# Gate products and squares of the first branch group moved into the last sampled sequence, and four first halves of the last down products ahead of the second halves, in a hybrid MLA and Mamba-2 decoder layer

## The reference, cut to what matters

```python
# sampled sequences: attention over 4096 cached positions, in the latent space
o_lat = (einsum('bhtk,bkc->bthc', p_past, past_ckv) + einsum('bhts,bsc->bthc', p_new, c_kv_new))
o = einsum('bthc,chd->bthd', o_lat, w_uv)
# Mamba-2 branch: gate, then RMS norm in 4 groups of 512 features
yg = (y * silu(z)).reshape(B, T, SSM_GROUPS, D_INNER // SSM_GROUPS)
yg = rms_norm(yg, ssm_norm_g, 1e-5)
merged = g_a * (attn @ w_branch_a) + g_b * (ssm_out @ w_branch_b)
mix = merged @ w_out
h = layer_norm(ALPHA * x + mix, ln1_g, ln1_b)
# feed-forward network and the last norm
y = layer_norm(ALPHA * h + (silu(h @ w_gate) * (h @ w_up)) @ w_down, ln2_g, ln2_b)
```

## Time and profile before

| | before |
|---|---|
| median of 3 runs | 2912.71 us (2912.24 to 2912.79) |
| the profiled execution's own time | 2923.22 us |
| its span, first to last instruction | 2921.4 us |
| PE busy | 2829.9 us, 97% of the span |
| DVE busy | 1477.7 us, 51% |
| ACT, POOL busy | 736.8 us and 1015.3 us, 25% and 35% |
| mean granted TensorE clock | 0.979 of full speed |

### The profile page before, as it was taken

How to read it: one execution, slowest core, us unless ns; L and a number is a source line. 1 busy time by engine, 2 the same in 40 slices (tenths; PEclk the granted TensorE clock), 3 DMA queues, 4 the chain that set the end, 5 groups by cost and what they waited for, 6 DMA issues and landing times.

```text
span 2921.4 us, 45631 instructions
## 1 busy us (share of the span) xinstructions
PE 2829.9 (97%) x18894; PEld 2533.1 (87%) x18894; DVE 1477.7 (51%) x2052; ACT 736.8 (25%) x1154; POOL 1015.3 (35%) x603
## 2 busy tenths in 40 slices
PE   7999999999999999999999889999899999999998
PEld 7999999899999984555766589999799999999997
DVE  3535778766666655555344347865652222222226
ACT  2111211454454544454323222010120000000000
POOL 3443334333333314444211123444333333333331
PEclk9999999999999998999999989999899999999999
DMA  4263223565656544222343334353211111111111
GB/s 142 73 197 119 81 85 121 177 168 150 173 162 171 147 138 120 65 65 69 148 184 129 116 129 140 111 182 106 66 37 44 44 45 49 43 43 50 43 50 60
DMA packets 314769, 309.72 MB, mean 106 GB/s; under 512 B 32101, under 2 KB 273002, under 8 KB 312138
## 3 DMA queue, kind: packets, MB, share of 16 engines
q1 hardware_dynamic: 252392, 196.02, 23.7%
q10 hardware_dynamic: 58650, 73.89, 7.5%
q0 software_dynamic: 3584, 37.75, 3.4%
HBM read 229.41 MB, written 78.20 MB: 105 GB/s over the span
## 4 chain that ended last, share of the span: by engine, by line
PE 81%; DVE 11%; ACT 3%; issue 3%; DMA 1%; POOL 1%; ACTq 0%; SPq 0%; POOLq 0%; DVEq 0%
PE ps L969 41%; PE ps L1150 12%; PE ps L1284 4%; DVE cv L2237 3%; PE ps L1308 2%; PE ps L1298 2%; PE ps L1442 2%; PE ps L1418 2%; PE ps L1398 2%; DVE cv L2231 1%; PE ps L1183 1%; PE ps L1187 1%; PE ps L1176 1%; PE ps L1647 1%; DVE cv L2239 1%
## 5 line engine op out<-in xcount | busy, mean ns | idle before, releaser
L776 POOL TENSOR_TENSOR whi<-raw,cst 128x1024 fp32r<-128x1024 f32 x160 | 311.2, 1945 | 1154.1 <-PE ps L969 945.1
L778 POOL TENSOR_TENSOR wlo<-raw,whi 128x1024 fp32r<-128x1024 f32 x160 | 433.0, 2706 | 12.5
L969 PE MATMUL ps<-ahi,whi 128*128 128x352 f32 x1728 | 375.7, 325 | 2.1 <-POOL wlo L778 1.4
L969 PE MATMUL ps<-alo,whi 128*128 128x352 f32 x1728 | 375.9, 326 | 0.0
L969 PE MATMUL ps<-ahi,wlo 128*128 128x352 f32 x1728 | 372.6, 324 | 0.0
L969 PEld LDWEIGHTS ps<-ahi,whi 128*128 128x128 f32 x1728 | 294.7, 189 | 2.7 <-POOL wlo L778 1.7
L969 PEld LDWEIGHTS ps<-ahi,wlo 128*128 128x128 f32 x1728 | 296.9, 190 | 0.0
L969 PEld LDWEIGHTS ps<-alo,whi 128*128 128x128 f32 x1728 | 295.7, 189 | 0.0
L1150 PE MATMUL ps<-xhi,whi 128*128 128x352 f32 x768 | 255.9, 333 | 0.4 <-ACT xraw L1751 0.4
L1150 PE MATMUL ps<-xhi,wlo 128*128 128x352 f32 x768 | 247.9, 323 | 0.0
L1150 PE MATMUL ps<-xlo,whi 128*128 128x352 f32 x768 | 247.7, 323 | 0.0
(11 more groups left out here) (368 smaller groups left out, 5034.0 us busy)
## 6 DMA issues: line engine op xcount, KB each, us to landing
raw<-in_w_in SPq DMA_DIRECT2D x61, 512.0 KB, 5.0
s_a<-d_acum SPq DMA_DIRECT2D x32, 512.0 KB, 7.3
d_xbc<-so ACTq DMA_DIRECT2D x24, 528.0 KB, 2.7
gt<-d_g SPq DMA_DIRECT2D x24, 528.0 KB, 3.6
raw<-in_w_ffn_gate SPq DMA_DIRECT2D x22, 512.0 KB, 3.8
raw<-in_w_ffn_up SPq DMA_DIRECT2D x22, 512.0 KB, 3.7
raw<-in_w_ffn_down SPq DMA_DIRECT2D x22, 512.0 KB, 3.5
d_z<-zo ACTq DMA_DIRECT2D x16, 528.0 KB, 4.8
```

The source lines that it names most:

```text
L776: pool.tensor_tensor(whi[s][:, :], raw[:, u], ones[:, 0:1].broadcast_to([P, UNIT]), ALU.mult).then_inc(sem("unit_hi"), k["unit_hi"].adds(1))
L778: pool.tensor_tensor(wlo[s][:, :], raw[:, u], whi[s][:, :].bitcast(F32), ALU.subtract).then_inc(sem("unit_split"), k["unit_split"].adds(1))
L969: last = pe.matmul(ps[0:m, 3 * b + c, 0:width], w(j), x[:, j, at:at + width], start=i == 0, stop=i == n - 1)
```

## The change

The gate products of the first group are made by DVE inside the last sequence, after its copies of `prt` and before it waits for `olat_ready`; the sums of squares are taken right after `oseq`, before it waits for `end_turned`. So that the squares have room while `prt` is still read, `prt` and `oseq` lie further up in memory, and ACT waits with the fourth square (`murow`, which still lies over `prt`) for the eighth `olat_ready`. In the tail TensorE makes the first half (weight unit 0) of the token tiles 0 to 3 before it waits for the second weight unit, and the waits for free banks stand apart, ahead of the tiles that need them.

```diff
@@ memory
-    prb, prt = ar("prb", [P, NBK + 1, P]), ar("prt", [P, NBK + 1, P])
+    prb = ar("prb", [P, NBK + 1, P])
+    at_prt = ar.at + 704
+    ar = Arena(at_prt)
+    prt = ar("prt", [P, NBK + 1, P])
     oseq = ar("oseq", [P, NB, KL])
@@ PE, tail
-        def last_down(i):
+        def last_half(i, s):
             n = P if i < 8 else NS
             at, bank = slice(i * P, i * P + n), (6, 0, 2, 4)[i % 4]
-            if i >= 4:
-                pe.wait_ge(sem("tile_read"), k["tile_read"].next())
-            for s in range(2):
-                if i == 0:
-                    pe.wait_ge(sem("unit_split"), k["unit_split"].next())
-                for m in range(6):
...
-            if i == 0:
-                for b in range(2):
-                    pe.wait_ge(sem(f"res_free{b}"), k[f"res_free{b}"].next())
...
+        pe.wait_ge(sem("unit_split"), k["unit_split"].next())
+        last_half(0, 0)
+        pe.wait_ge(sem("res_free0"), k["res_free0"].next())
+        last_half(1, 0)
+        last_half(2, 0)
+        pe.wait_ge(sem("res_free1"), k["res_free1"].next())
+        last_half(3, 0)
+        pe.wait_ge(sem("unit_split"), k["unit_split"].next())
         for i in range(9):
-            last_down(i)
+            if i >= 4:
+                pe.wait_ge(sem("tile_read"), k["tile_read"].next())
+                last_half(i, 0)
+            last_half(i, 1)
+            sum_onto(i)
@@ ACT, squares
                 act.wait_ge(sem(f"yt_free{j % 2}"), k[f"yt_free{j % 2}"].next())
+                if g == 0 and j == 3:
+                    act.wait_ge(sem("olat_ready"), NB)
                 act.activation(sq4[j], yz[:, j], ACT.Square)...
@@ DVE, in sequence(b, q, more)
+            if not more and stop >= 7:
+                gated(0, 4)
             dve.wait_ge(sem("olat_ready"), k["olat_ready"].next())
@@ DVE, after the last sequence
+        if stop >= 7:
+            add_pairs()
+            add_all()
         dve.wait_ge(sem("end_turned"), k["end_turned"].next())
...
-        if stop >= 7:
-            gated(0, 4)
-            add_pairs()
-            add_all()
         dve.wait_ge(sem("os_ready"), k["os_ready"].next())
```

More of the change, by code:

```diff
@@ L438, in build @@
     assert ar.at >= at_g
+    assert ar.at + 3 * TOK * 4 <= at_prt
     srow, sq2, murow, rsrow = ar("srow", [P, TOK]), ar("sq2", [P, 2, TOK]), ar("murow", [P, TOK]), ar("rsrow", [P, TOK])
@@ L1633, in _, with sum_onto @@
         pe.wait_ge(sem("f_split"), k["f_split"].next(2))
-        def last_down(i):
+        def last_half(i, s):
             n = P if i < 8 else NS
             at, bank = slice(i * P, i * P + n), (6, 0, 2, 4)[i % 4]
-            if i >= 4:
-                pe.wait_ge(sem("tile_read"), k["tile_read"].next())
-            for s in range(2):
-                if i == 0:
-                    pe.wait_ge(sem("unit_split"), k["unit_split"].next())
-                for m in range(6):
-                    j, part = divmod(m, 3)
-                    w, x = ((whi, fhi), (whi, flo), (wlo, fhi))[part]
-                    pe.matmul(ps[0:n, bank + s, :], x[:, j, at], w[s][:, j * 512:(j + 1) * 512], start=m == 0, stop=False)
-            if i == 0:
-                for b in range(2):
-                    pe.wait_ge(sem(f"res_free{b}"), k[f"res_free{b}"].next())
+            for m in range(6):
+                j, part = divmod(m, 3)
+                w, x = ((whi, fhi), (whi, flo), (wlo, fhi))[part]
+                pe.matmul(ps[0:n, bank + s, :], x[:, j, at], w[s][:, j * 512:(j + 1) * 512], start=m == 0, stop=False)
+        def sum_onto(i):
+            n = P if i < 8 else NS
+            at, bank = slice(i * P, i * P + n), (6, 0, 2, 4)[i % 4]
             for e in range(KT):
@@ L2509, in keys_out, with gated @@
             dve.tensor_copy(dst, ps[:, 4 + i % 3, :].rearrange("p (r n) -> p r n", n=P)).then_inc(sem("keys_read1"), k["keys_read1"].adds(1))
+        def gated(j0, j1):
+            for j in range(j0, j1):
+                dve.wait_ge(sem(f"yt_full{j % 2}"), k[f"yt_full{j % 2}"].next(32))
+                dve.tensor_tensor(yz[:, j], yt[j % 2][:, :], gt[j % 2][:, :], ALU.mult).then_inc(sem(f"yt_free{j % 2}"), k[f"yt_free{j % 2}"].adds(1))
         def sequence(b, q, more):
@@ L2559, in _ @@
         sequence(1, NB - 1, False)
[L2560 to L2564, removed]
         def add_pairs():
```

## The result

| | before | after |
|---|---|---|
| median | 2912.47 us (2909.58 to 2912.79, 4 runs) | 2894.70 us (2890.39 to 2900.22, 4 runs) |
| ratio | | 0.9939, 95% interval 0.9926 to 0.9951 |
| the profiled execution's own time | 2923.22 us | 2900.22 us |
| its span | 2921.4 us | 2898.4 us |
| mean granted TensorE clock | 0.979 | 0.980 |

The changed kernel is 17.8 us faster (14.3 to 21.5). Later comparisons on four other chips gave less than 17.8, as the experiments show. In two of them the changed kernel has one disturbed execution (3290 us in after_again, 10144 us in after_third), which medians and ratios leave out.

What follows compares the result with a forecast made beforehand. TensorE, busy 97% of the span, was taken as the bound, with gains only where it waits or runs at lower clock. Hand-over 8.5 plus tail 2.6 makes 11.1 us, from 2912.7 to 2901.6 us; range 2895.5 to 2905.5.

Steps and rivals of the forecast that it cites:

- The base: Starting time: median 2912.7 us, with the profiled execution 10.5 us above it; gains carried over unchanged.
- Step 1: Hand-over, VectorE's order: the division waits behind the fourth gate product and its load, starting 1.5 us later.
- Step 2: Hand-over at full clock: the half unit ends at 1685.2 instead of 1699.06, a gain of 13.8 us.
- Step 3: Hand-over, TensorE's clock: falls about the middle of L1480, costing 5.25 us, so the first part gains 8.5 us.
- sign for a fallen clock: In the changed profile, L1480's count of 32 takes 4.5 to 6 us if the clock fell.
- Rival A: The clock holds through the hand-over: gain 16.4 us, time 2896.3 us; chance 0.20.
- Passed on whole: Behind the half unit everything waits by the same distances, so the shift reaches the end whole; 1.7 us either way for clock.
- Step 4: Tail: first halves fill the 3.12 us wait, then DVE sets the pace at 4.28 us a tile; gain 2.6 us.
- B: Less is passed on: clock down longer (hand-over gains 4, not 8.5) or tail keeps its pace; 2904 to 2908 us; chance 0.21.
- C: Hand-over: the fourth tile lands late and DVE holds up everything behind it; slower than before; chance 0.02.
- D: Hand-over: first two tiles not there at 1657.6, or additions wait for ACT's last square; 2910.1 us; chance 0.04.

Runs made afterwards that it cites:

- after_again: The changed kernel, nothing edited, run again on chip 9: median 2908.26 us, ratio 0.9954 to the kernel before.
- after_third: The changed kernel, nothing edited, run again on chip 4: median 2907.18 us, ratio 0.9953 to the kernel before.
- fourth_later: The changed kernel with the fourth gate product behind the division and two of three additions behind the copies of olat: 2899.17 us, ratio 0.9928 to before.
- after_fourth: The changed kernel, nothing edited, run again on chip 1: median 2895.08 us, ratio 0.9949 to the kernel before.
- after_fifth: The changed kernel, nothing edited, run again on chip 15: median 2895.34 us, ratio 0.9951 to the kernel before.
- before_filled: The kernel before plus 48 unread matmuls ahead of the group's sums, where TensorE idles: median 2913.87 us, ratio 1.0008 to the kernel before.
- fourth_later2: The kernel of fourth_later, nothing edited, run again on chip 1: median 2897.66 us, ratio 0.9956 to the kernel before.
- first_only: The kernel before with only the hand-over changed (gate products, additions, memory, ACT's wait), tail as before: median 2910.88 us, ratio 0.9963.
- before_again: The kernel before, nothing edited, run again on chip 15: median 2911.81 us, ratio 1.0002.
- memory_only: The kernel before with only prt and oseq moved further up in memory: median 2921.49 us, ratio 1.0002.
- after_filled: The changed kernel with eight and four unread matmuls in TensorE's two hand-over gaps: median 2906.44 us, ratio 0.9954 to the kernel before.

## Why the prediction was right or wrong

**The base.** The profile of before came from an execution with 30.0 us per sequence, its three timed runs have the median of chips with 28.4. That fits most of the 10.5 us between them (medians of the two kinds of chip differ by 9 to 10.6), which the prediction left unexplained and carried over unchanged. This was right, since neither place lies in the sequences' repeated part.

**Step 1, the order of VectorE.** Right in kind. The fourth tile landed 1655.44 - 1645.94 = 9.5 us after the first product's start (forecast 9.6). The division was 1.0 us late in the first profile and 0 to 1.2 in the six, where 1.5 was forecast. The Trainium skill (TensorE: Matmul & The Clock Gate, section Architectural detail: the array is 16× 32×32, not 1× 128×128) calls VectorE's queue strict first-in, first-out; the trace agrees, the division started only behind the waiting product, and fourth_later, which moves that product, has it start at once.

**Step 2, full clock.** Right. It gave 13.8 us with a division 1.5 late. In after_fourth and after_fifth, in which the clock held from the sums up to the half unit, 13.7 and 12.9 are gained. The division was 1.5 and 0.8 us less late than forecast there, and the half unit lost 1.5 in each (7.6 instead of 6.1), so with both set right it is 13.7 and 13.6.

**Step 3, the clock.** This is the step that failed. One price, 5.25 us, was put to a matter that comes out differently in each execution. In the first profile L1484 lost 7.09 - 3.79 = 3.3 us, more than the upper bound of 2.2; that bound took a ratio of 1.68 from L1432, the last of whose matmuls had run at full clock, where half clock costs 1.87 times. (Its sign for a fallen clock, 4.5 to 6 us for L1480's matmuls, was too low by the same.) L1490 lost 1.57 (forecast 1.2), the sums 3.68 - 2.04 - 0.75 = 0.9 (1.25; the 0.75 is the idle time behind them in after_fourth), the half unit 8.24 - 6.1 = 2.1 (1.7). That is 7.9 instead of 5.25. With 0.5 less delay the step gives 13.8 + 0.5 - 7.9 = 6.4; the trace has 6.3. But after_third lost only 4.7, and two of six profiles lost nothing between the sums and the half unit, and 1.5 in all (after_fourth had lost 2.1 before the sums, as two profiles of the order before do). By the same count the six lost 1.5 to 7.9, in the mean 4.7: the mean was forecast well, the spread was not in the sum. The mean gain of 9.6 is 1.1 above the forecast of 8.5, half of it from a division that was 0.9 late in the mean and not 1.5. Rival A, that the clock holds, was no rival to be decided: it is one outcome of the same kernel, and had a chance of 0.20 where two profiles of six show it up to the half unit. Its reason was not enough either: behind a short gap the clock fell in before_filled and fourth_later2.

**Passed on whole.** Partly wrong, and nothing in the sum or the range stood for it but 1.7 us of clock. From the half unit's end to the tail, the order before needs 1167.6 to 1169.7 us (four profiles; before_filled, with its pauses, 1176.2), the changed one 1168.2 to 1175.1 (six), 2.9 more in the mean. Three of the changed kernel's five profiles have a loss in the fourth group that no profile of the order before shows. In after_fifth:

```profile
1799.45 2.95 DVE L2586 TENSOR_TENSOR sq<-sq 128x1056 f32<-128x1056 f32 x1
...
1801.37 3.29 POOL L782 TENSOR_TENSOR wlo<-raw,whi 128x1024 fp32r<-128x1024 f32 x1
1802.33 3.45 DVE L2586 TENSOR_TENSOR srow<-srow,murow 128x1056 f32<-128x1056 f32 x1
...
1809.89 3.65 PE L1506 MATMUL ps<-cst,sq 128*88 128x1 f32 x24 [4.93 <-DVE sq L2590]
```

Both additions fall on POOL's split of a weight unit and take 2.95 and 3.45 us instead of 1.25; TensorE waits 4.93 us and then runs the sums at half clock. In after_fourth the first addition is ahead of the split:

```profile
1800.24 1.25 DVE L2586 TENSOR_TENSOR sq<-sq 128x1056 f32<-128x1056 f32 x1
...
1801.41 2.95 DVE L2586 TENSOR_TENSOR srow<-srow,murow 128x1056 f32<-128x1056 f32 x1
...
1809.18 2.01 PE L1506 MATMUL ps<-cst,sq 128*88 128x1 f32 x24 [2.61 <-DVE sq L2590]
```

The difference is 4.93 - 2.61 + 3.65 - 2.01 = 4.0 us. That the shifted timing of the load (the third and fourth product wait for it) decides between the two was not tried. The Trainium skill (SBUF — State Buffer, section Who interferes with whom) says that a VectorE instruction with two inputs in SBUF contends with a GpSimd instruction that reads SBUF, and that the order of issue decides who is held up. The durations agree with this: in after_fourth the addition that began first kept its 1.25 us.

**Step 4, the tail.** The mechanism was right: no wait for the second unit, and VectorE leading from the first tile on. The first tile came 0.5 us earlier, as forecast, and this was partly luck: it is so beside a profile of before whose clock had fallen behind the wait, and beside first_only and before_again, where it held, the new order's first tile is 0.8 us later. The pace was mis-sized: forecast 4.28 us a tile with a step of 0.03 between tiles, measured 4.16, since the next tile's first operation starts 2861.54 + 1.28 - 2862.74 = 0.08 before the end of the last. Eight times 0.12 is the 1.0 us by which the tail brought 3.7 instead of 2.6.

**Rivals.** B held in part for single executions (6.3 instead of 8.5) but not in the mean. C fell: the load landed when forecast. D fell: the tiles were there.

**The number and the range.** By all five comparisons the change is worth 14.9 us, which from the base of 2912.7 would be 2897.8; by each of the four later ones alone it would be 2897.8 to 2899.3. All of these are in the range, and the first comparison drew a faster set. What made it miss is step 3: the range, with its lower end at 2895.5, has rival A's 2896.3 just inside it and nothing for executions that lose less than 5.25 us of clock and have the better tail. With the gain of 13.7 us that after_fourth shows in the hand-over and 3.7 in the tail the sum would be 2912.7 - 17.4 = 2895.3. Three of the four executions of the first comparison had a mean granted clock of 0.985 to 0.986 and took 2890.4 to 2894.8 us, the profiled one 0.980 and 2900.2. That the three kept the clock in the hand-over fits this, and is not shown, since they have no profile. About 1 us of the miss is the tail and 1 the hand-over; the rest is how executions scatter: fifteen runs of the kernel before on one chip spread over 8.8 us, where the three on record at the prediction lay within 0.55.

Profiles give less than times: from the start of the last values' product to the end of the span the five profiles of the changed kernel need 11.1 us less in the mean than before, memory_only and before_again, against 14.9. A part of this is which executions were profiled. All five of the changed kernel were slower than the median of their set, by 2.6 us in the mean, and before_again's was 2.4 us faster. The rest remains open.

## What to carry to other kernels

Work that waits for a load, and whose inputs are there long before its turn, belongs ahead of the wait for the engine that leads; look what is queued behind it in order, since it may hold that up, and where a delay pushes later two-input operations of VectorE against GpSimd's. Where the trace has a fall of TensorE's clock, treat its place and price as a spread over executions, not as a value: one profile and three runs don't show it, and a fix "proved" by one session may vanish in the next. Matmuls that nothing reads are no neutral test of it, since a longer program had pauses elsewhere. When one stage before the change takes another time in the two profiles, run the unchanged kernel again before reading anything into it.

## What the runs showed of the hardware

- TensorE's clock fell in every one of the sixteen profiles between the last turning of the probabilities (behind idle time of 1.99 us) and the first half unit, mostly more than once. Behind that turning it was still down in the last values' product four times (8.96 to 9.23 us instead of 7.13, in memory_only, before_again, after_fourth and after_filled), whatever the order. Further on it fell in L1480 or L1484 (4.65 to 7.09 instead of 3.79), in L1490 (3.65 instead of 2.08), in the idle time ahead of the sums (L1502 3.65 instead of 1.97, four profiles of the order before), or only in the half unit (7.4 to 7.6 instead of 6.1). Gaps ahead of L1484 of 2.0 to 2.2 us went with a fall in it four times out of four; after one of 1.67 it held; after one of 0.97 it fell once in nine, in before_filled. The Trainium skill (TensorE: Matmul & The Clock Gate, section What's actually happening) calls the rise of the clock at a kernel's start run-variable; in these profiles the places where it falls differ between executions of one kernel as well.
- Behind 3.1 us of idle time ahead of the second weight unit the next six matmuls of 128x512 ran at half clock in two profiles of five, from the third on in one, and at full clock in two.
- The three kernels with unread matmuls, and none of the thirteen others, had pauses of 0.65 to 2.39 us in the feed-forward part, some 600 us and more behind the added matmuls, in which nothing in the profile is waited for.
- Two kinds of session: 64 matmuls over 32 rows took 1.34 us on two chips and about 3.0 on two others, with the same program; the medians of the kernel before differ by 9 to 10.6 us between them.
- An addition of two 128x1056 float32 tensors took 1.25 us alone and 2.95 to 3.45 beside GpSimd's split of a weight unit, whose second part took 3.29 instead of 2.34.
- Two independent operations of VectorE overlap by some 0.08 us in the profile where nothing stands between them (the end at 2861.54 + 1.28 and the start at 2862.74 above).
